# Three late slots of each expert layer gathered by two indirect DMAs, of 120 and 8 rows

## The reference, cut to what matters

```python
def peer(xn, ...):                       # of both blocks, for 128 tokens at a time
    ...                                  # e: (token, 8 heads, 16) indices of experts; g: their weights
    ue = jnp.take(u, e, axis=0)          # rows of 1024 float32
    ve = jnp.take(v, e, axis=0)          # rows of 1024 float32
    act = jax.nn.gelu(jnp.einsum('thkd,td->thk', ue, xb), approximate=False)
    return jnp.einsum('thk,thkd->td', (g * act), ve)
```

## Time and profile before

| | us |
|---|---|
| median of 3 runs | 1953.31 (1952.21 to 1957.02) |
| the profiled execution | 1956.59 |
| its span, first to last instruction | 1954.8 |
| PE busy | 1687.4 (86%) |
| DVE busy | 1299.2 (66%) |
| ACT busy | 927.4 (47%) |
| POOL busy | 831.0 (43%) |
| software DMA queue (gathers and other GpSimd DMAs) | 67.0% of 16 engines |
| SyncE's DMA queue | 14.4% of 16 engines |

### The profile page before, as it was taken

The page is one execution under the profiler, slowest core; times in us unless marked ns, Lnnn a source line. Parts: engine busy times, 40 slices in busy tenths (PEclk is TensorE's granted clock), DMA queues, the critical chain, the costliest instruction groups (busy, mean ns, idle before and its releaser), DMA issues.

```text
span 1954.8 us, 22622 instructions
## 1 busy us (share of the span) xinstructions
PE 1687.4 (86%) x7638; PEld 1038.4 (53%) x7638; DVE 1299.2 (66%) x2808; ACT 927.4 (47%) x2424; POOL 831.0 (43%) x756
## 2 busy tenths in 40 slices
PE   7998988877787788799899999999988877778777
PEld 7996444422332222399899999974444222222222
DVE  4568877666776664558845784488767666666644
ACT  5456554444544444466524344465454444444443
POOL 3335433433333333277615475654434333333331
PEclk9999999999999999999999999999999999999999
DMA  7548999999999999654303324779999999999996
GB/s 252 188 155 331 422 421 421 421 421 421 421 421 421 422 421 421 266 163 151 108 22 97 120 92 138 266 300 421 421 420 421 422 421 422 422 421 422 421 421 286
DMA packets 102053, 637.61 MB, mean 326 GB/s; under 512 B 11264, under 2 KB 12544, under 8 KB 36144
## 3 DMA queue, kind: packets, MB, share of 16 engines
q0 software_dynamic: 75216, 543.73, 67.0%
q1 hardware_dynamic: 26720, 92.43, 14.4%
HBM read 635.07 MB, written 1.05 MB: 325 GB/s over the span
## 4 chain that ended last, share of the span: by engine, by line
PE 42%; DMA 35%; DVE 12%; ACT 8%; issue 2%; POOL 1%; SPq 0%; DVEq 0%; ACTq 0%; POOLq 0%
DMA arena<-in_uv,arena 31%; PE pb L657 18%; PE pb L397 6%; PE pb L399 5%; PE pb L398 5%; DVE arena L1817 3%; DMA spare<-in_uv,arena 3%; ACT arena L1112 3%; PE pb L476 1%; PE pb L872 1%; DVE parts L1385 1%; PE pb L794 1%; PE pb L785 1%; ACT parts L958 1%; ACT arena L1107 1%
## 5 line engine op out<-in xcount | busy, mean ns | idle before, releaser
L657 PE MATMUL pb<-arena 128*128 128x512 f32 x1904 | 930.5, 619 | 211.5 <-ACT arena L1112 210.7
L1817 DVE SCALAR_TENSOR_TENSOR arena<-arena,pb 128x1024 f32<-128x1024 f32 x476 | 580.6, 1220 | 373.5 <-DMA arena<-in_uv,arena 373.3
L2324 POOL DMA_INDIRECT arena<-in_uv,arena x476 | 452.7, 951 | 725.5 <-PE pb L657 690.3
L657 PEld LDWEIGHTS pb<-arena 128*128 128x128 f32 x1904 | 331.7, 191 | 771.5 <-ACT arena L1112 517.5
L2298 POOL TENSOR_TENSOR parts<-ring,parts 128x512 fp32r<-128x512 f32 x222 | 330.4, 1511 | 311.9 <-ACT parts L958 310.9
L1104 ACT ACTIVATE arena<-arena 128x1 f32<-128x1 f32 x512 | 103.2, 201 | 585.6 <-DVE arena L1817 539.1
L958 ACT ACTIVATE parts<-ring 128x512 fp32r<-128x512 f32 x300 | 180.4, 627 | 174.4 <-PE pb L399 151.7
L397 PE MATMUL pb<-xl,parts 128*128 128x256 f32 x704 | 220.0, 313 | 12.1 <-POOL parts L2298 5.4
L1112 ACT ACTIVATE arena<-cst,arena 128x128 f32<-128x128 f32 x512 | 205.5, 401 | 48.3 <-ACT arena L1107 1.9
L399 PE MATMUL pb<-xh,parts 128*128 128x256 f32 x704 | 201.3, 286 | 0.0
L398 PE MATMUL pb<-xh,parts 128*128 128x256 f32 x704 | 201.3, 286 | 0.0
(11 more groups left out here) (329 smaller groups left out, 1682.9 us busy)
## 6 DMA issues: line engine op xcount, KB each, us to landing
ring<-in_w_in SPq DMA_DIRECT2D x108, 512.0 KB, 3.5
ring<-in_wq SPq DMA_DIRECT2D x18, 512.0 KB, 4.1
ring<-in_w_out SPq DMA_DIRECT2D x16, 512.0 KB, 3.8
arena<-in_uv,arena POOLq DMA_INDIRECT x476, 20.1
arena<-in_wq SPq DMA_DIRECT2D x10, 512.0 KB, 5.2
ring<-in_wa SPq DMA_DIRECT2D x8, 512.0 KB, 3.6
ring<-in_wb SPq DMA_DIRECT2D x8, 512.0 KB, 3.7
spare<-in_wq SPq DMA_DIRECT2D x4, 512.0 KB, 4.8
```

What stands on the lines that cost most here:

```text
L657: ins = pe.matmul(ys[hf][:, :], diags[:, k % 4, :], lands[land_of[k]][:, D + hf * 512:D + (hf + 1) * 512], start=False, stop=k % (8 * K) = ...
L1817: ve.scalar_tensor_tensor(z, z, 1.0, xg[t], ALU.mult, ALU.mult, accum_out=hidden[:, k:k + 1]).then_inc(*up("v_dot", ("dot", e, k)))
L2324: gp.indirect_dma_start(lands[land_of[k]], None, rows_uv, bass.IndirectOffsetOnAxis(ap=eidx[:, k:k + 1], axis=0)).then_inc(*up(f"dma_rows{ ...
```

## The change

The list `SPLIT` names three slots of each layer. For these GpSimd issues two indirect DMAs in place of one: first the last 8 rows, for partitions 120 to 127, then the first 120. Both count on the landing area's semaphore, and the dot waits for both. The indices of an indirect DMA are given from partition 0 on, so the 8 rows need their indices in partitions 0 to 7: a small DMA of SyncE moves the 8 by 16 block of batch 13 (512 bytes) there, into a part of the same scratch region that nothing else uses. GpSimd waits for that DMA ahead of the first split slot. SyncE issues it once a layer, after a wait for the indices of batch 13: in layer 1 right ahead of the wait for the last gather, in layer 2 after the last weight load and ahead of the output stores. All other gathers stay as they are.

```diff
+SPLIT = (208, 210, 212)
...
+        eidx_of_last = rest[0:8, 64:80].bitcast(U32)
...
-                    gp.indirect_dma_start(lands[land_of[k]], None, rows_uv,
-                                          bass.IndirectOffsetOnAxis(ap=eidx[:, k:k + 1], axis=0)).then_inc(
+                    n = P
+                    if k in SPLIT:
+                        n = 120
+                        gq.wait_ge(*on(("eidx_of_last", e)))
+                        gp.indirect_dma_start(lands[land_of[k]][n:P, :], None, rows_uv,
+                                              bass.IndirectOffsetOnAxis(ap=eidx_of_last[:, k % K:k % K + 1], axis=0)).then_inc(
+                            *up(f"dma_rows{land_of[k]}", None, 16))
+                    gp.indirect_dma_start(lands[land_of[k]][0:n, :], None, rows_uv,
+                                          bass.IndirectOffsetOnAxis(ap=eidx[0:n, k:k + 1], axis=0)).then_inc(
                         *up(f"dma_rows{land_of[k]}", ("rows", e, k), 16))
...
         def sync_program(sq, sp):
+            def last_indices(e):
+                j = SPLIT[0] // K
+                sq.wait_ge(*on(("eidx", e, j)))
+                sp.dma_start(eidx_of_last, eidx[120:P, j * K:(j + 1) * K]).then_inc(*up("dma_eidx", ("eidx_of_last", e), 16))
...
                 if (name, i) == ("w_in2", 0):
+                    last_indices(1)
                     sq.wait_ge(*on(("rows", 1, NT * 8 * K - 1)))
                 sp.dma_start(ring_of(k), d[name][i]).then_inc(*up(f"w_slot{ring_no[k] % SLOTS}", None, 16))
+            last_indices(2)
             for t in range(NT):
```

## The result

The changed kernel takes 1984.02 us in the median of 4 runs (1982.42 to 1991.89), the kernel before beside it 1954.21 us (4 runs): a ratio of 1.0158, 95% interval 1.0143 to 1.0173. It is slower by about 30 us, where 1953.3 us and "same" were forecast. The profiled execution took 1991.89 us (span 1990.1, 35.3 more than the span before); it lies 7.9 us above its median, so the trace has some 5 us more to explain than the medians.

The account below looks back on a forecast made before the run. DMA gathers bound the expert stages, each layer ending on one late engine. No bytes saved and every added issue, wait and DMA at 0 left the kernel before's time, 1953.3 us; 8-in-10 range 1945.9 to 1956.3.

Parts of the forecast that it names:

- same: Whole kernel: a change within about 0.3% (5.86 us), which a measurement can't tell from none; chance 0.79.
- Bytes: Gathers of three slots a layer: same rows fetched, only the engine moving them may change; 6.35 us less to 1.87 more.
- The mechanism of the bound: Expert stages: gathers set the pace, so a gain or loss at the last landing passes through to the end unshrunk.
- GpSimd: Three more indirect issues a layer, 0.94 us each, and three waits, hidden by some 14 us of queued gathers: 0.
- The small DMA and its wait: Index DMA of 512 B ahead of slot 208: it has 35 us to land, so the wait costs 0.
- SyncE: Its new wait and issue cost 0; in layer 2 the stores of tile 0 move from 1656.14 to about 1771.
- Not relieved: Layer ends: the late engine keeps about its share of rows; 1953.3 us, range 1950.8 to 1955.2, chance 0.52.
- a tail that is gone: Layer ends: the last 3.15 and 3.20 us of one engine alone vanish, layer 1's last transfer ending near 809, not 812.2.
- a wait of GpSimd at slot 208: First split slot of a layer: GpSimd held up by the index DMA, where no wait was forecast.
- a small gather whose issue outlasts the queue: Short gathers on GpSimd: an issue longer than the queued gathers cover, where near 0.94 us was forecast.
- The slower rival: Layer ends: the eight rows all go to the second-late engine; 8.6 us more, 1961.9 us, chance 0.05.
- 0.06 for slower: Whole kernel: the chance given to a measurably slower result, beyond about 0.3% (5.86 us).

Follow-up runs that it names:

- 120 at 4: Kernel before with 24 slots in a row gathering only 120 rows, from partition 4 on, other rows left out: 0.59 us a row.
- 96 at 16: Kernel before with 24 slots in a row gathering only 96 rows, from partition 16 on, other rows left out: 0.56 us a row.

## Why the prediction was wrong, step by step

**Bytes: the step that failed.** It took from whole gathers that "a row costs it 8192 B / 26.3 = 0.311 us", used this price for gathers of every shape, and then asked only which engine moves the row. All its bounds, 6.35 us less to 1.87 us more, are prices of that question. While the 120-row gathers and the whole ones queued beside them are under way, a row costs 0.62 us in the mean of all 16 engines; that is 31.8 us in the trace (16.6 and 15.2), about the 30 measured. All 512 gathers of the trace had one shape, as the step itself said: it had a row for who is late, and none for what another shape costs. A dearer row was put at nothing without a reason, and the range left no room for it.

**The mechanism of the bound was right.** The gathers set the pace, so the rate lost in the stretches comes out at the end unshrunk: 16.6 us lost and 2.2 of longer tail make 18.8 of the 19.3 us by which the layer's end moved.

**GpSimd: right, 0.** The 8-row issues take 0.87 to 0.90 us, the 120-row ones 0.96 to 1.00 in both layers, where 0.94 was taken; the gap ahead of slot 208 is 2.14 us, 2.06 before. The later gaps of 5 us follow from late landings. Six more issues for even and odd halves cost nothing either.

**The small DMA and its wait: right, 0.** It was issued at 639.22, 35 us ahead of slot 208; with it and the waits alone the time was 1.0002 of the kernel before.

**SyncE: right.** The stores of tile 0 moved from 1656.14 to 1791.04, which is the forecast of about 1771 and the 19.3 us by which all of layer 2 came later; nothing waits for them.

**Not relieved: right as far as the tails tell, and of no weight.** Neither tail is gone: 4.50 and 2.30 us of one engine alone remain, where 3.15 and 3.20 give or take 0.9 were forecast. Layer 2 is at the edge of that and layer 1 above it, on the side away from relief. Which engine gets none of the 120 rows can't be read from the trace.

**The signs of being wrong missed it.** The prediction named three: a tail that is gone, a wait of GpSimd at slot 208, a small gather whose issue outlasts the queue. None of them came, and the time was still 30 us off, since none of the three looks at the rate of the transfers.

**The slower rival had the right sign and another mechanism.** It priced 24 rows too many on one engine, 8.6 us; what came was a half rate of all sixteen for some 32 us a layer. That the sign agrees is luck. With 0.06 for slower the chances leaned on the trace's showing nothing against the price of a row, which is not the same as showing it.

## What to carry to other kernels

A gather's price per row holds for its own shape: before one of other partitions is put into a stage that DMA bounds, time it by itself, and let the bound reach to at least twice the price until that is done. Where a slot must be split, the 64 even and the 64 odd partitions were the one split that was free here; 120 and 8 rows, and 112 and 16, were not. Equal numbers of rows in both halves of the partitions are not enough (120 at 4 and 96 at 16 were slow). One oddly shaped transfer costs more than its own rows, since whole ones queued beside it slow down with it.

## What the runs showed of the hardware that was not expected

- A busy share of 1.0 is no sign of the full rate: the engines showed 1.02 at 216 GB/s and 1.01 at 421.
- The same 64 rows a gather ran at 205 GB/s on partitions 0 to 63, at a share of 1.00, and at 302 GB/s on the 64 even ones with the share at 0.89 and PE full.
- One slot gathered as 120 and 8 rows among whole ones slowed 16 us of transfers; three such slots within five slowed 36 us.
- While the gathers were slow, the granted clock of TensorE was 0.73 of full in the mean, so for a part of them it stood at the lower of its two levels (1.2 and 2.4 GHz), with 19.49 us of PE work in 32. It was 0.74 from 720 to 740 us, while the gathers were back at 415 GB/s.
